# Input sums of the seven-product MLP moved from VectorE to GpSimd, their rests placed elsewhere

## The reference

```python
def sqrelu_mlp(h, w_up, w_down):
    a = jax.nn.relu(h @ w_up)
    return (a * a) @ w_down

def reference(x, ...):
    for i in range(DEPTH):          # DEPTH = 2
        ...
        h = rmsnorm(x, norm_mlp[i])
        x = x + sqrelu_mlp(h, mlp_w_up[i], mlp_w_down[i])
    return rmsnorm(x, norm_final)
```

## Time and profile before

| | |
|---|---|
| median of 3 runs | 1074.43 us (1074.08 to 1074.49) |
| profiled execution | 1074.78 us, its span 1073.0 us |
| TensorE busy | 1051.8 us, 98%, 6088 matmuls |
| VectorE busy | 800.7 us, 75%, 1124 instructions |
| ScalarE busy | 558.9 us, 52% |
| GpSimd busy | 81.7 us, 8%, 132 instructions |
| granted TensorE clock | 0.997 of 2.4 GHz |
| transfers | 155.30 MB, 145 GB/s on average |

### The profile page before, as it was taken

How to read it: one execution, slowest core, us unless ns; L and a number is a source line. 1 busy time by engine, 2 the same in 40 slices (tenths; PEclk the granted TensorE clock), 3 DMA queues, 4 the chain that set the end, 5 groups by cost and what they waited for, 6 DMA issues and landing times.

```text
span 1073.0 us, 15173 instructions
## 1 busy us (share of the span) xinstructions
PE 1051.8 (98%) x6088; PEld 911.7 (85%) x6088; DVE 800.7 (75%) x1124; ACT 558.9 (52%) x781; POOL 81.7 (8%) x132
## 2 busy tenths in 40 slices
PE   9999999998999999999999999999998999999996
PEld 8888888987998998988887777779887988988984
DVE  5876688599788698598426666636699698697696
ACT  6122256564574674576424444426563674674663
POOL 2452000000000000000110000000000000000000
PEclk9999999999999999999999999999999999999998
DMA  7994264035745745642454323152054647457432
GB/s 241 382 354 143 79 157 137 21 84 192 197 118 159 195 118 172 182 118 60 136 156 143 108 84 107 60 235 80 1 118 172 182 118 206 148 137 201 133 74 83
DMA packets 32245, 155.30 MB, mean 145 GB/s; under 512 B 5232, under 2 KB 5360, under 8 KB 20656
## 3 DMA queue, kind: packets, MB, share of 16 engines
q1 hardware_dynamic: 21600, 102.80, 27.0%
q0 software_dynamic: 10576, 51.54, 20.4%
HBM read 113.80 MB, written 10.48 MB: 116 GB/s over the span
## 4 chain that ended last, share of the span: by engine, by line
PE 90%; DVE 6%; DMA 2%; issue 1%; SPq 1%; ACT 1%; DVEq 0%; POOL 0%; POOLq 0%; ACTq 0%
PE bank L588 28%; PE bank L590 28%; PE bank L589 28%; DMA raw<-weights 2%; PE bank L786 2%; DVE w_l L1175 2%; PE bank L768 1%; PE bank L753 1%; PE bank L611 1%; DVE xs L1329 1%; DVE sx L1254 1%; SPq L481 1%; PE bank L801 0%; DVE big L1229 0%; DVE big L1219 0%
## 5 line engine op out<-in xcount | busy, mean ns | idle before, releaser
L908 ACT ACTIVATE w_h<-big 128x1024 fp32r<-128x1024 f32 x210 | 221.6, 1058 | 224.3 <-PE bank L590 224.2
L588 PE MATMUL bank<-a_h,w_h 128*128 128x256 f32 (+1 forms) x896 | 297.1, 332 | 2.5 <-DVE w_l L1175 2.5
L589 PE MATMUL bank<-a_l,w_h 128*128 128x256 f32 (+1 forms) x896 | 294.6, 329 | 0.0
L590 PE MATMUL bank<-a_h,w_l 128*128 128x256 f32 (+1 forms) x896 | 294.6, 329 | 0.0
L1175 DVE TENSOR_TENSOR w_l<-big,w_h 128x1024 fp32r<-128x1024 f32 x210 | 250.0, 1216 | 26.7 <-ACT w_h L908 23.7
L588 PE MATMUL bank<-w_h,hx 128*128 128x512 f32 x568 | 222.9, 392 | 5.7 <-DVE w_l L1175 5.7
L589 PE MATMUL bank<-w_l,hx 128*128 128x512 f32 x568 | 221.1, 389 | 0.0
L590 PE MATMUL bank<-w_h,hx 128*128 128x512 f32 x568 | 221.1, 389 | 0.0
L588 PEld LDWEIGHTS bank<-a_h,w_h 128*128 128x128 f32 x896 | 170.5, 190 | 20.8 <-issue 6.1
L590 PEld LDWEIGHTS bank<-a_h,w_l 128*128 128x128 f32 x896 | 170.5, 190 | 15.2
L589 PEld LDWEIGHTS bank<-a_l,w_h 128*128 128x128 f32 x896 | 170.5, 190 | 15.0 <-issue 0.2
(11 more groups left out here) (142 smaller groups left out, 1176.3 us busy)
## 6 DMA issues: line engine op xcount, KB each, us to landing
big<-blocks SPq DMA_DIRECT2D x56, 1024.0 KB, 4.9
raw<-weights SPq DMA_DIRECT2D x68, 512.0 KB, 3.6
big<-big POOLq DMA_DIRECT2D x30, 1024.0 KB, 7.2
bias_tiles<-big POOLq DMA_DIRECT2D x8, 624.0 KB, 9.1
big<-bias_tiles POOLq DMA_DIRECT2D x8, 624.0 KB, 4.1
big<-blocks POOLq DMA_DIRECT2D x4, 1024.0 KB, 26.1
bias_tiles<-bias_rows POOLq DMA_DIRECT2D x48, 64.0 KB, 11.7
big<-x SPq DMA_DIRECT2D x8, 256.0 KB, 4.9
```

Of the source, the lines that this page charges most:

```text
L588: nc.tensor.matmul(dst, sh, mh, start=start, stop=False, skip_group_check=again)
L589: nc.tensor.matmul(dst, sh, ml, start=False, stop=False, skip_group_check=again)
L590: return nc.tensor.matmul(dst, sl, mh, start=False, stop=stop, skip_group_check=again)
L908: nc.scalar.activation(wh_all[:, w % SLOTS, :], src, ACT.Copy).then_inc(w_hi, 1)
```

## The change

GpSimd computes the four input sums; VectorE's `in_sums` is gone. A new semaphore `in_step` makes each GpSimd step wait for the one before it. GpSimd's program is put in a new order: sums 1 to 3 of an MLP stand ahead of the two adds t3 and t4 of that MLP's first down matrix, sum 4 right behind them. ScalarE's `in_round` 1 and 2 move up behind units U5 and U6, 3 to P6 of the down product, 4 into the next chunk's up product; VectorE's rests 1 and 2 move up behind U6 and U7, 3 to P7, 4 into the next chunk's up product.

```diff
+            def in_raw(n, i, name, step):
+                pool.tensor_tensor(sum_raw[i], u_part(name, False).bitcast(f32), u_part(name, True).bitcast(f32),
+                                   ALU.add).then_inc(in_step, 1)
+                pool.wait_ge(in_step, 5 * n + step)
+
+            def input_sums(n):
+                t0, t1 = sum_raw
+                pool.wait_ge(a_ready, a_place(2 * n + 1, 1) + KT)
+                in_raw(n, 0, "P3", 1)
+                in_raw(n, 1, "P4", 2)
+                pool.tensor_tensor(t1, t0, t1, ALU.add).then_inc(in_sum, 1)
...
+                pool.wait_ge(in_lo, 4 * n + 2)
+                in_raw(n, 0, "P1", 4)
+                pool.tensor_tensor(t1, t0, t1, ALU.subtract).then_inc(in_sum, 1)
+
+            def input_sums_late(n):
+                t0, t1 = sum_raw
+                pool.wait_ge(in_sum, 4 * n + 3)
+                in_raw(n, 0, "P2", 5)
+                pool.tensor_tensor(t0, t0, t1, ALU.add).then_inc(in_sum, 1)
...
-            for q in range(SEQ_ATTN):
-                add_sums(q)
...
+            add_sums(0)
+            for n in range(2):
+                input_sums(n)
+                add_sums(7 * n + 1)
+                input_sums_late(n)
+                for q in range(7 * n + 2, 7 * n + 8):
+                    add_sums(q)
+                if n == 0:
+                    attention()
...
@@ scalar, up_seven @@
                     elif pos == 2:
                         nc.scalar.activation(X_BLOCK["X21"], up_pair("P6"), ACT.Copy).then_inc(up_copy, 1)
+                        if c == 1:
+                            in_round(n, 3)
@@ scalar, second @@
-                        if tc and pos in (1, 4, 5):
-                            for i in {1: (0, 1), 4: (2,), 5: (3,)}[pos]:
-                                in_round((tc - 1) // CHUNKS, i)
+                        if tc and pos == 2:
+                            in_round((tc - 1) // CHUNKS, 2)
@@ scalar, mlp @@
+                    if m in (5, 6):
+                        in_round(n, m - 5)
@@ vector, second @@
-                        if tc and pos in (2, 5, 6):
-                            for i in {2: (0, 1), 5: (2,), 6: (3,)}[pos]:
-                                in_rest((tc - 1) // CHUNKS, i)
-                        if tc and pos in (3, 4):
-                            in_sums((tc - 1) // CHUNKS, pos)
+                        if tc and pos == 4:
+                            in_rest((tc - 1) // CHUNKS, 2)
@@ vector, mlp @@
-                        in_sums(n, m - 5)
+                    if m > 5:
+                        in_rest(n, m - 6)
```

More of the change, by code:

```diff
@@ L385, in encoder @@
         adds = sem("adds")
+        in_step = sem("in_step")
         in_sum = sem("in_sum")
@@ L535, in load_bias, with attention @@
                 pool.dma_start(head_bias[j % 2], bias_dram[:, 2 * j:2 * j + 2, :]).then_inc(bias_in[j % 2], 16)
+            def attention():
+                pool.wait_ge(w_split, second_first(CHUNKS) + 14)
+                pool.memset(v_shift[3][HD:P, :], 0.0).then_inc(shift_zero, 1)
+                for half in range(2):
+                    pool.wait_ge(v_got, 4 * (half + 1))
+                    f = slice(512 * half, 512 * half + 512)
+                    for s in range(4):
+                        if s:
+                            pool.dma_start(v_shift[s - 1][HD:P, f], v_tile[s][0:HD, f]).then_inc(v_in, 16)
+                        pool.dma_start(v_shift[s][0:HD, f], v_tile[s][HD:P, f]).then_inc(v_in, 16)
+                pool.wait_ge(tiles_in, 16 * 3 * WIN)
+                pool.wait_ge(tr_done, 16)
+                for j in range(KT):
+                    load_bias(j)
+            def in_raw(n, i, name, step):
[8 more added lines that the diff above has]
+                pool.tensor_tensor(t1, t0, t1, ALU.add).then_inc(in_sum, 1)
+                pool.wait_ge(in_sum, 4 * n + 1)
+                pool.tensor_tensor(t0, t0, u_part("P1", False).bitcast(f32), ALU.subtract).then_inc(in_step, 1)
+                pool.wait_ge(in_step, 5 * n + 3)
+                pool.tensor_tensor(t0, t0, u_part("P1", True).bitcast(f32), ALU.subtract).then_inc(in_sum, 1)
+                pool.wait_ge(in_lo, 4 * n + 2)
[6 more added lines that the diff above has]
+                pool.tensor_tensor(t0, t0, t1, ALU.add).then_inc(in_sum, 1)
             pool.memset(ones[:], 1.0).then_inc(const_ready, 1)
@@ L1225, in sums_of_y @@
                     nc.vector.tensor_tensor(room[at["T2"]], room[at["Y12"]], room[at["Y22"]], ALU.subtract).then_inc(t_sum, 1)
[L1227 to L1250, removed]
             def in_rest(n, i):
@@ L1290, in up_seven @@
                     lo(first + 2 * pos + 3)
+                    if c == 1 and pos == 3:
+                        in_rest(n, 3)
                     if pos == 5:
```

## The result

The changed kernel takes 1081.43 us (median of 4 runs, 1081.00 to 1082.09) against 1074.46 us of the kernel before in the same runs: ratio 1.0065, 95% interval 1.0053 to 1.0078. It is 7.0 us slower; the forecast was 1085.5 us, 11.1 us slower, in a range of 1075 to 1089. The profiled execution took 1081.25 us, its span 1079.5 us against 1073.0.

What follows compares the result with a forecast made beforehand. The prediction took VectorE's weight rests and the landing of Y11's load as the bounds; 2 x 5.4 us plus 0.3 for the early sums gave 11.1 us slower, 1085.5 us after allowing for the profiled run's offset, range 1075 to 1089.

Steps and rivals of the forecast that it cites:

- The bound and the possible gain: Both MLPs: VectorE's weight rests and Y11's load bound the stage; removing all TensorE waits brings at most 7.7 us.
- The price of a sum: Each input sum on GpSimd, reading two operands, was taken at 2.2 us, with 0.93 us kept for the range.
- Turn by turn: MLP stage: VectorE's two-SBUF-input instructions and GpSimd's sums shut each other out for whole instructions; likeliest case, 51%.
- The turns at D3 to D4: Start of the down product: GpSimd's two sums alternate with VectorE's small rests, ending D4's rest at 241.3.
- the wait of 3.5 us that I put at D4: Down product: TensorE wants D4 at 237.8 but its weight rest ends at 241.3, a new 3.5 us wait.
- Y12's load: Goes out at 239.0 and runs beside both adds, so t4 lands 4 us later, at 255.5.
- the 5.4 us per MLP: Next chunk's up product, N0, starts at 275.1 instead of 269.74, 5.4 us later in each MLP.
- the five early sums: Sums 1 and 2, before 219.9: hidden by VectorE's lead of some 5 us, 0.3 us in the total.
- The late block alone: Rival: engines don't disturb each other, only Y11 comes late; +1.5 us, 1076 us (1075 to 1077.5), 28%.
- The faster case: Rival: adds overlap more or a GpSimd sum takes 0.93 us; N0 2.6 us early per MLP, 1069 us, 8%.
- sums and rests in new places: The fourth rest and ScalarE's four roundings, moved elsewhere, cost nothing; 1 us if the cover is gone.

Runs made afterwards that it cites:

- experiment 6: Kernel before the change, all nine sums kept on VectorE but moved to other places, GpSimd as before: 1067.15 us, ratio 0.9935.
- experiment 3: Changed kernel with fills in place of GpSimd's sums, and t3 and t4 ahead of sum 3: 1066.09 us, ratio 0.9922 to the kernel before.
- experiment 2: Changed kernel with GpSimd's nine sums replaced by fills that read nothing, t3 and t4 still behind sum 3: 1078.07 us, ratio 1.0033.
- experiment 5: Changed kernel with each GpSimd sum replaced by two linked copies of its first operand, t3 and t4 ahead of sum 3: 1069.97 us, ratio 0.9956.
- experiment 4: Kernel before the change, sums on VectorE, with t3 and t4 of each MLP's first down matrix made to wait until about 240: 1084.96 us, ratio 1.0096.

## Why the prediction came out as it did

**The bound and the possible gain: right.** VectorE's row of weight rests and the landing of Y11 bound the stage, and 7.7 us was the most to be had: experiment 6 got 7.3, experiment 3, with less work, 8.4; inside the MLPs, by the rows, 8.2 and 7.8, so the bound was some 0.5 us low at most.

**The price of a sum: right within a tenth.** Taken at 2.2 us, measured 2.40 alone. Another figure for it is the Trainium skill's (GPSIMD Engine Reference, Elementwise — side-by-side cycle accounting), 4497 ns for 2048 elements; an estimate from it is half, 2.25 us, and the rows show slightly more, 2.40.

**Turn by turn: right, and shown.** Experiments 2, 3 and 5 separate reading from writing. The Trainium skill's rule (SBUF — State Buffer, Who interferes with whom) holds here wherever an experiment touched it: 3.43 us beside a sum, 2.05 us beside a copy, 1.22 us beside a fill, and 1.21 us for an eviction beside a copy. Who got the turn was another matter, as the next paragraph shows.

**The turns at D3 to D4: wrong in order.** I let GpSimd come in between VectorE's small rests. In the trace the sum that was ready at 232.91 got its turn only at about 234.6, when VectorE came to an eviction; a weight rest and two small ones went ahead of it. So the wait of 3.5 us that I put at D4 was spread over D4 to D7, 3.1 us.

**Y12's load: the term that was mis-sized.** By the same slip I had the small rests done at 239.0 and Y12's load beside both adds, 4 us more for t4. Measured: the rests were done at 234.6, the load went out at 234.67 and had landed before the adds started. t4 took 11.4 us from its issue at 240.78 (I had 15.9), Y11's sum began at 257.27 and not at 260.4, and the MLP lost 3.1 us less for it. This makes the 5.4 us per MLP 2.3. Two terms came on top: the five early sums cost 0.7 us per MLP at U5, where I had 0.15, and the clock 1.4 us in the first MLP, which I had at nothing. I had said that VectorE's weight rests were some 5 us early there; the three rows of VectorE from 198.74 to 209.13 lasted 6.6 us longer than without a neighbour, which is more than that cover. Together 4.4 and 2.8 us against 5.4 twice and 0.3; that the clock is nearly the whole difference between the two MLPs is read from the rows and was not tried by itself.

**The rivals.** The late block alone, taken at 1.5 us, measured 3.6 us in experiment 2. By the rows the clock, which I had at nothing, took all of that, so without it the block eats the gain of 7.7 us and costs nothing beyond, where I had +1.5 us. Its mechanism was right; set against the case with free turns and early adds it is a cause of 12.0 us, some 8 of them the block itself. The faster case would have needed early adds and free turns, and neither was there. That sums and rests in new places cost nothing was right.

## What to carry to other kernels

Work moved to GpSimd is only off VectorE when GpSimd's instruction reads nothing, as the fills here, or VectorE's has an operand in PSUM, as the eviction: a sum that costs VectorE 1.13 us cost it up to 2.3 us as a neighbour. Before a second engine is called in, look where the first one sits idle: gaps of 4.9 and 2 us took sums 1 to 3 almost whole, and sum 4 found room in the next up product. And what is put in front of a transfer's issue in an in-order queue must be followed to who waits for the landing, here two transfers, a load and a sum further on.

## What the runs showed of the hardware that was not expected

- GpSimd's turn does not come in the order of asking: an instruction ready at 232.91 was passed by two that VectorE began at 233.88 and later. From 235.69 on, where VectorE had one 128x1024 instruction behind the other, GpSimd's turn came after each of them.
- The clock fell to 1.2 GHz behind waits of 2.36 us (first MLP, changed kernel), 4.3 and 5.4 us, and not behind 2.17, 1.6 and 1.4 us. It came back after 7 to 14 matmuls at 0.43 us. Whether it costs anything depends on what the stage waits for: by the rows 1.4 us in the changed kernel, nearly 4 us in experiment 2, next to nothing in experiment 4.
- Two adds of 1 MB issued 0.6 us apart landed at 247.2 and 252.2, 5.0 us apart, against the 5.7 us of the earlier trace rows.
